# Convolution norm: channel tiles added on VectorE before the ones product, and another order of work around the attention projection

## The reference

```
u = ua * sigmoid(ub)                                  # 256 x 1024
u = causal_depthwise_conv(u, conv_w, conv_b)          # 31 taps per channel
mu  = mean(u, over the 1024 channels)                 # one number per token
var = mean(square(u - mu), over the channels)
u = silu((u - mu) * rsqrt(var + 1e-6) * g + b)
y_a = u @ w_conv_out
...
o = attention(...)                                    # 8 heads
y_b = o @ w_attn_out
return (g_a * y_a + g_b * y_b) @ w_out
```

## Time and profile before

| | us |
|---|---|
| median of 3 runs | 1172.5 |
| lowest and highest | 1171.62, 1177.98 |
| the profiled execution | 1175.44 |
| its span, from the first to the last instruction | 1171.9 |
| TensorE busy | 1121.5 (96%) |
| VectorE busy | 819.3 (70%) |
| ScalarE busy | 562.2 (48%) |
| GpSimd busy | 42.0 (4%) |
| mean granted TensorE clock | 0.995 |

### The profile page before, as it was taken

One profiled execution on the slowest core, in us unless ns is written; L12 is line 12 of the kernel. 1 busy time (PEld: TensorE's weight loads), 2 busy tenths in 40 slices (PEclk: granted clock), 3 DMA queues, 4 the chain that ended last, 5 costly groups with the idle time before them and its releaser, 6 DMA issues.

```text
span 1171.9 us, 20666 instructions
## 1 busy us (share of the span) xinstructions
PE 1121.5 (96%) x8488; PEld 951.2 (81%) x8488; DVE 819.3 (70%) x1161; ACT 562.2 (48%) x709; POOL 42.0 (4%) x48
## 2 busy tenths in 40 slices
PE   8999999999999796899999999999999999999997
PEld 7888888889778586787888887788878888999996
DVE  3565444548498565969999987899997777555554
ACT  4535543445564435364434455354465655444443
POOL 0000000000001310101111000000000000000000
PEclk9999999999999999999999999999999999999999
DMA  9386556543343111569999953464441354564632
GB/s 324 112 258 206 177 189 215 179 165 129 102 141 115 41 22 40 182 207 329 348 336 358 324 194 106 119 198 149 149 144 37 109 184 142 176 211 147 214 111 105
DMA packets 129219, 204.88 MB, mean 175 GB/s; under 512 B 11176, under 2 KB 86717, under 8 KB 129150
## 3 DMA queue, kind: packets, MB, share of 16 engines
q1 hardware_dynamic: 121716, 176.58, 45.8%
q0 software_dynamic: 6560, 25.19, 6.2%
q10 hardware_dynamic: 874, 2.12, 0.5%
HBM read 201.78 MB, written 1.05 MB: 173 GB/s over the span
## 4 chain that ended last, share of the span: by engine, by line
PE 77%; DVE 13%; ACT 4%; issue 3%; DMA 2%; SPq 0%; ACTq 0%; DVEq 0%
PE ps L681 21%; PE ps L683 21%; PE ps L682 21%; DVE wl L2404 4%; DVE wide L3083 2%; PE ps L1074 2%; DMA raw<-in_ffn_w_up 2%; PE ps L758 1%; PE ps L891 1%; ACT wh L1669 1%; PE ps L987 1%; PE ps L1545 1%; PE ps L1106 1%; PE ps L1379 1%; PE ps L986 1%
## 5 line engine op out<-in xcount | busy, mean ns | idle before, releaser
L2404 DVE TENSOR_TENSOR wl<-raw,wh 128x2048 fp32r<-128x2048 f32 (+3 forms) x156 | 349.8, 2248 | 132.7 <-ACT wh L1669 132.5
L681 PE MATMUL ps<-wh,xh 128*128 128x512 f32 (+4 forms) x1112 | 411.0, 370 | 13.0 <-DVE wl L2404 5.4
L683 PE MATMUL ps<-wl,xh 128*128 128x512 f32 (+4 forms) x1112 | 402.5, 362 | 0.0
L682 PE MATMUL ps<-wh,xl 128*128 128x512 f32 (+4 forms) x1112 | 402.3, 362 | 0.0
L1669 ACT ACTIVATE wh<-raw 128x2048 fp32r<-128x2048 f32 (+3 forms) x156 | 290.6, 1881 | 86.1 <-PE ps L683 66.8
L681 PEld LDWEIGHTS ps<-wh,xh 128*128 128x128 f32 x1112 | 210.5, 189 | 50.5 <-issue 7.5
L683 PEld LDWEIGHTS ps<-wl,xh 128*128 128x128 f32 x1112 | 210.5, 189 | 32.4
L682 PEld LDWEIGHTS ps<-wh,xl 128*128 128x128 f32 x1112 | 210.9, 190 | 31.2 <-issue 1.0
L681 PE MATMUL ps<-wh,gh 128*128 128x512 f32 x280 | 109.7, 392 | 1.2 <-DVE wl L2404 0.8
L682 PE MATMUL ps<-wh,gl 128*128 128x512 f32 x280 | 109.1, 390 | 0.0
L683 PE MATMUL ps<-wl,gh 128*128 128x512 f32 x280 | 109.0, 389 | 0.0
(11 more groups left out here) (383 smaller groups left out, 1188.7 us busy)
## 6 DMA issues: line engine op xcount, KB each, us to landing
wide<-in_w_ada POOLq DMA_DIRECT2D x24, 1024.0 KB, 9.8
raw<-in_ffn_w_gate SPq DMA_DIRECT2D x44, 512.0 KB, 4.4
raw<-in_ffn_w_up SPq DMA_DIRECT2D x44, 512.0 KB, 5.5
raw<-in_ffn_w_down SPq DMA_DIRECT2D x22, 1024.0 KB, 5.4
raw<-in_w_mlp_in SPq DMA_DIRECT2D x16, 1024.0 KB, 7.1
raw<-in_w_mlp_out SPq DMA_DIRECT2D x16, 1024.0 KB, 5.1
raw<-in_w_in SPq DMA_DIRECT2D x16, 512.0 KB, 5.0
raw<-in_w_in SPq DMA_DIRECT2D x8, 1024.0 KB, 5.1
```

What stands on the lines that cost most here:

```text
L681: pe.matmul(o, lh, rh, start=start, stop=False)
L682: pe.matmul(o, ll, rh, start=False, stop=False)
L683: return pe.matmul(o, lh, rl, start=False, stop=stop)
L2404: v.tensor_tensor(wl[:, s, 0:width], raw[:, s, 0:width], f32(wh[:, s, 0:width]), ALU.subtract).then_inc(lo_ready[s], 1)
```

## The change

On TensorE the eight ones products for the mean become one, and so do the eight for the squares. VectorE adds the eight tiles first, in a tree of three instructions (4 tiles + 4 tiles, 2 + 2, 1 + 1) that leaves the sum in `sq[:, 0, :]`; the first tree reads `cv`, the second the squares, in place. After each of the first two additions VectorE waits for its own instruction (`link`). TensorE waits for `cv_sum` 1 and 2. The mean product stands earlier, between the two weight blocks of c = 0, the product for the squares where it was.

On VectorE the first tree stands ahead of the low part of attn_out (1,0); the second stands behind that of attn_out (1,1), with `attention_gated(0)` behind it; the low part of conv_out (0,0) moves behind the multiplication by the reciprocal. On ScalarE one small SiLU instruction and the high part of conv_out (0,1) stand right behind the root, ahead of the wait for the normalised tiles. `cv_sum` shares a semaphore that existed already.

```diff
             def conv_mean():
                 pe.wait_ge(S("at.xl"), B("at.xl") + NH)
-                order = [(kt, STEPS_OF[kt]) for kt in range(KT)]
-                for n, (kt, steps) in enumerate(order):
-                    if steps:
-                        pe.wait_ge(S("conv_step"), B("conv_step") + steps)
-                    else:
-                        pe.wait_ge(S("conv_pe"), B("conv_pe") + kt - (KT - CONV_PE) + 1)
-                    m = pe.matmul(ps[:, 4, 0:SEQ], ones[:, :], cv[:, kt, :], start=n == 0, stop=n == KT - 1)
-                m.then_inc(S("cmean"), 1)
+                pe.wait_ge(S("cv_sum"), B("cv_sum") + 1)
+                pe.matmul(ps[:, 4, 0:SEQ], ones[:, :], sq[:, 0, :], start=True, stop=True).then_inc(S("cmean"), 1)
 
             def conv_var():
-                for kt in range(KT):
-                    if kt % 4 == 0:
-                        pe.wait_ge(S("csq"), B("csq") + kt // 4 + 1)
-                    m = pe.matmul(ps[:, 5, 0:SEQ], ones[:, :], sq[:, kt, :], start=kt == 0, stop=kt == KT - 1)
-                m.then_inc(S("cvar"), 1)
+                pe.wait_ge(S("cv_sum"), B("cv_sum") + 2)
+                pe.matmul(ps[:, 5, 0:SEQ], ones[:, :], sq[:, 0, :], start=True, stop=True).then_inc(S("cvar"), 1)
...
                 half(s, range(2, 4), o, 512, False, False, 2).then_inc(w_used[s], 1)
+                if c == 0:
+                    conv_mean()
                 s = arrive(("attn_out", c, 1))
...
-                half(s, range(4, 6), o, 512, False, False)
-                if c == 0:
-                    conv_mean()
-                half(s, range(6, 8), o, 512, False, True, 2).then_inc(w_used[s], 1)
+                half(s, range(4, 8), o, 512, False, True).then_inc(w_used[s], 1)
...
@@ ScalarE
             act.activation(lowr[:, 256:512], lowr[:, 256:512], ACT.Sqrt).then_inc(S("cv_std"), 1)
+            act.activation(unused, eps, ACT.Silu)
+            split(("conv_out", 0, 1))
...
-                if k == 0:
-                    split(("conv_out", 0, 1))
...
@@ VectorE
             conv(len(taps))
+            sq = W3(5, KT)
+
+            def tile_sum(first):
+
+                for n in (4, 2, 1):
+                    src = cv if n == 4 and first else sq
+                    m = v.tensor_tensor(sq[:, 0:n, :], src[:, 0:n, :], src[:, n:2 * n, :], ALU.add)
+                    if n > 1:
+                        link(m)
+                m.then_inc(S("cv_sum"), 1)
+
+            v.wait_ge(S("conv_step"), B("conv_step") + 7 * CK)
+            v.wait_ge(S("conv_pe"), B("conv_pe") + CONV_PE)
+            v.wait_ge(S("at.o"), B("at.o") + NH)
+            tile_sum(True)
             split(("attn_out", 1, 0))
...
-            split(("attn_out", 1, 1), ("conv_out", 0, 0))
+            split(("attn_out", 1, 1))
+            v.wait_ge(S("csq"), B("csq") + 2)
+            tile_sum(False)
...
+            attention_gated(0)
             v.wait_ge(S("cvar"), B("cvar") + 1)
...
-            attention_gated(0)
+            split(("conv_out", 0, 0))
```

More of the change, by code:

```diff
@@ L209 @@
     "dve_35": (("wkv.r4d", 4), ("post1.add", 4)),
-    "dve_36": (("wkv.q", 4),),
+    "dve_36": (("wkv.q", 4), ("cv_sum", 2)),
     "dve_37": (("state", 4), ("pre2.hn", 4)),
@@ L1577, in ao_free @@
                     pe.wait_ge(S("at.sc"), B("at.sc") + 2 * NH)
-            cv, sq = W3(2, KT), W3(5, KT)
+            sq = W3(5, KT)
             def conv_mean():
                 pe.wait_ge(S("at.xl"), B("at.xl") + NH)
-                order = [(kt, STEPS_OF[kt]) for kt in range(KT)]
-                for n, (kt, steps) in enumerate(order):
-                    if steps:
-                        pe.wait_ge(S("conv_step"), B("conv_step") + steps)
-                    else:
-                        pe.wait_ge(S("conv_pe"), B("conv_pe") + kt - (KT - CONV_PE) + 1)
-                    m = pe.matmul(ps[:, 4, 0:SEQ], ones[:, :], cv[:, kt, :], start=n == 0, stop=n == KT - 1)
-                m.then_inc(S("cmean"), 1)
-            def conv_var():
-                for kt in range(KT):
-                    if kt % 4 == 0:
-                        pe.wait_ge(S("csq"), B("csq") + kt // 4 + 1)
-                    m = pe.matmul(ps[:, 5, 0:SEQ], ones[:, :], sq[:, kt, :], start=kt == 0, stop=kt == KT - 1)
-                m.then_inc(S("cvar"), 1)
+                pe.wait_ge(S("cv_sum"), B("cv_sum") + 1)
+                pe.matmul(ps[:, 4, 0:SEQ], ones[:, :], sq[:, 0, :], start=True, stop=True).then_inc(S("cmean"), 1)
+            def conv_var():
+                pe.wait_ge(S("cv_sum"), B("cv_sum") + 2)
+                pe.matmul(ps[:, 5, 0:SEQ], ones[:, :], sq[:, 0, :], start=True, stop=True).then_inc(S("cvar"), 1)
             ao_free(0)
@@ L3242, in _ @@
             attention_gated(0)
+            v.wait_ge(S("cvar"), B("cvar") + 1)
+            v.tensor_scalar(lowr[:, 256:512], ps[:, 5, 0:SEQ], 1.0 / D, EPS, ALU.mult, ALU.add).then_inc(S("cv_ss"), 1)
+            v.wait_ge(S("cv_std"), B("cv_std") + 1)
+            link(v.reciprocal(lowr[:, 768:1024], lowr[:, 256:512]))
+            for k in range(2):
+                o = slice(4 * k, 4 * k + 4)
+                v.tensor_tensor(cv[:, o, :], cv[:, o, :], lowr[:, 768:1024].unsqueeze(1).to_broadcast([P, 4, SEQ]), ALU.mult).then_inc(S("cv_n"), 1)
+            split(("conv_out", 0, 0))
             for k in range(2):
```

## The result

| | before | after |
|---|---|---|
| median, 19 runs each | 1173.82 us | 1167.71 us |
| lowest and highest | 1169.28, 1179.35 | 1163.38, 1175.13 |
| span of the profiled execution | 1171.9 us | 1169.8 us |
| mean granted clock | 0.995 | 0.993 |

With more runs the median of before is 1173.8 rather than the 1172.5 from which the forecast started.

What follows compares the result with a forecast made beforehand. TensorE's own work was taken as the bound, with the norm's chain close behind. TensorE's work shrinks 5.92 us, but the chain lets the convolution projection start 5.3 us earlier: 1172.5 - 5.3 = 1167.2 us, range 1165.8 to 1170.5 (8 in 10).

Steps and rivals of the forecast that it cites:

- TensorE's own work: Mean and squares groups in the attention projection: 3.46 us each becomes 0.50, removing 5.92 us in all (5.7 to 6.1).
- The trees: VectorE's three linked additions per tree, priced from profile rows of the same sizes: 2.42 us a tree.
- rival 4: VectorE becomes the bound: additions of 2.29 us each make the second sum late, 1175.6 us; chance 0.06.
- The cover of the second sum: Second tree's sum ready at 912.2 us, TensorE wants it at 912.91: 0.7 us to spare.
- The chain: Norm's chain from mean through variance, root and SiLU to the convolution projection, which starts 5.3 us earlier, at 922.9.
- the first rival: More gain: slot 2 frees sooner or conv_out (0,1)'s high part doesn't hold SiLU; chain 0.7 us earlier, 1166.2 us; chance 0.13.
- The fifth rival: ScalarE stands still behind each table load for another 1.28 us, SiLU 1.65 us late, 1168.9 us; chance 0.04.
- The second rival: Clock falls after TensorE's 1.1 us wait ahead of the convolution projection, losing 1.7 us, 1168.9 us; chance 0.12.
- the third rival: A wait behind the stage, as for a block of w_out or loop weights, takes up the gain, 1172.5 us; chance 0.07.

Runs made afterwards that it cites:

- trees-only kernel: The changed kernel with all order edits undone, the two trees and single products kept; stage length 27.02 us against 24.13, ratio to before 0.9970.
- gating-first kernel: The changed kernel with the gating of c = 0 ahead of the second tree instead of behind it; stage length 25.43 us against 24.13.

## Why the prediction was right

**TensorE's own work.** Forecast 5.92 us, measured 6.02. The group costs 0.42, the lower bound of two steps of 0.216, not the 0.50 of the middle: there is no change-over. That the chain takes back most of the gain without the order is what the trees-only kernel shows (2.5 of 6.0 are left).

**The trees.** 2.42 forecast, 2.40 and 2.41 measured. The rows of the same sizes were the right ones, and rival 4, with each addition at 2.29, is out. The cover of the second sum, 0.7 forecast, is 0.65, and the gating-first kernel shows what lies behind it.

**The chain.** In times from the stage's start, forecast and measured: scaling of the mean +6.16 and +6.17; scaling of the variance +14.83 and +14.80; high part of conv_out (0,1) +17.7 and +17.62; SiLU +19.5 and +19.44; convolution projection +24.2 and +24.13; idle time 1.1 and 1.17. This rests on having seen that a moved instruction on ScalarE waits for a slot that TensorE frees late, and that SiLU waits behind it. Undoing the move gave 0.63 us, about the size of the first rival; in the changed kernel the instruction does block, so that rival didn't come true. A slip beside it changed nothing: against that rival the prediction names the 36th matmul behind 904.75 as the release, but its own sum (24, 12 and 12 steps) makes it the 48th.

**Table loads.** The fifth rival is out: behind the load at 917.81 the small instruction starts at 919.10, 0.01 us behind its end, and the root's load ends at 917.03, ahead of the root at 917.37. The drain of about 1.38 us beside each load, which the Trainium skill states (page "ScalarE: Activation LUTs", section "What ACT_TABLE_LOAD costs"), doesn't show here, ahead of a load as little as behind it: the root ends at 917.79 and the load follows at 917.81.

**The clock.** The second rival didn't come true in either profile of the changed kernel: 1.00 behind the 1.17 us. That is no proof that it can't, since behind the 1.39 us at 848 us, on which the rival leant, five profiles of 13 show a fall. The rival's price of 1.7 us was near: 1.3 to 1.5 there, 1.3 to 2.3 in the stage.

**Nothing given back.** 5.37 us at the convolution projection, 5.38 ahead of the feed-forward block, 5.5 at the end of the span: the third rival is out.

**What was off.** That the time came within 0.5 us of the forecast is in part luck. The forecast started from a median of three runs, 1172.5, which nineteen runs put at 1173.8, so 1.3 us too low; and the medians lie 6.1 us apart, 0.8 more than the 5.3 forecast. The two errors cancel but for 0.5. What bears the mechanism out is the stage's length, 5.37 against 5.3.

The chances are the weakest part. The prediction put 0.64 on a change that can't be told from none, because 5.3 us lie below the 5.9 that 0.5% makes. The ratio's middle, 6.3 us, lies above 5.9 and its interval on both sides, so the runs don't settle it. The prediction says that it puts a fifth to a quarter of its forecast beyond the bound, and then reckons with 0.3; a quarter would give 0.28 for faster and not 0.30. With a forecast 0.6 us from the bound and a base that was itself off by 1.3, both outcomes deserved nearly even chances.

## What to carry to other kernels

When work is taken off the engine that bounds a stage, make the sum twice: along that engine, and along the chain that ends last beside it. Here the first gave 6.0 us and the second 5.4, and without reordering the chain 2.5 were left.

An instruction moved forward into a gap brings its own wait along: ask which release it waits for, and what queues behind it; here one such move cost 0.63 us of the gain.

If two orders differ by less than the spread of runs, read lengths within the stage, from its own start, and look at the granted clock in the same stretch.

## What the runs showed of the hardware

A short group of two fp32 matmul records between projection matmuls costs two steps and nothing more, 0.42 us.

Identical code ahead of the stage took 894.2 to 902.1 us in 13 profiles, 8 us of spread, while the stage itself repeated within 0.05 us in the two kernels that were profiled twice.

The granted clock fell to the lower level, 1.2 GHz, behind idle times of 1.80, 2.88 and 4.07 us in this stage and cost 1.3 to 2.3 us each; behind 1.17 or 1.18 (five profiles), 1.95 (two) and 2.29 (one) it didn't. Behind one and the same idle time of 1.39 us it fell in five profiles of 13, the same kernel once with a fall and once without, and a fall cost 1.3 to 1.5 us. An edit that only lengthens a wait can thus cost more than the wait, and whether it does differs from execution to execution.
